# Attention stage: where the next pair's q and k products stand, and the order of copies in the last two pairs

## The reference

```python
q, k, v = jnp.split(x @ w_in, 3, axis=-1)          # 16 heads of 64
q = q * 64 ** -0.5
s = einsum('bihd,bjhd->bhij', q_c, k_c) + bias      # bias by clipped distance, per head
p = softmax(where(valid, s, NEG_INF))
o = einsum('bhij,bjhd->bihd', p, v_c)
return o @ w_out
h = layer_norm(ALPHA * h + y, g, b)
```

## Time and profile before

| What | Value |
| --- | --- |
| Median of three executions | 1161.33 us |
| Profiled execution, its own time | 1161.39 us |
| Its span, first to last instruction | 1159.6 us |
| TensorE busy | 1150.3 us (99%) |
| VectorE, ScalarE, GpSimd busy | 706.2, 525.5, 406.3 us (61, 45, 35%) |
| Chain that ended last, TensorE's share | 98% |
| Granted TensorE clock, mean | 0.999 of full |
| Attention scores, first and last start | 623.9 and 757.4 us |

### The profile page before, as it was taken

The page is one execution under the profiler, slowest core; times in us unless marked ns, Lnnn a source line. Parts: engine busy times, 40 slices in busy tenths (PEclk is TensorE's granted clock), DMA queues, the critical chain, the costliest instruction groups (busy, mean ns, idle before and its releaser), DMA issues.

```text
span 1159.6 us, 18903 instructions
## 1 busy us (share of the span) xinstructions
PE 1150.3 (99%) x6960; PEld 1020.4 (88%) x6960; DVE 706.2 (61%) x1178; ACT 525.5 (45%) x918; POOL 406.3 (35%) x240
## 2 busy tenths in 40 slices
PE   9999999999999999999999999999999999999997
PEld 7888888989999998888887878788999999998886
DVE  5070173789888873443504667757888888844436
ACT  4355253335555554332415565762355555543222
POOL 2539425141111115446145443551311111144441
PEclk9999999999999999999999999999999999999999
DMA  6533314242223334325032212141223333333221
GB/s 221 179 130 109 109 37 146 77 143 96 92 103 109 109 109 145 107 75 181 20 109 73 91 47 91 46 166 53 73 73 110 109 109 109 109 125 115 87 73 73
DMA packets 21976, 119.89 MB, mean 103 GB/s; under 512 B 2448, under 2 KB 6672, under 8 KB 8992
## 3 DMA queue, kind: packets, MB, share of 16 engines
q1 hardware_dynamic: 15440, 104.96, 25.6%
q10 hardware_dynamic: 6480, 14.17, 3.5%
HBM read 117.02 MB, written 5.24 MB: 105 GB/s over the span
## 4 chain that ended last, share of the span: by engine, by line
PE 98%; issue 0%; ACT 0%; DVE 0%; POOL 0%; DVEq 0%; POOLq 0%; ACTq 0%
PE bank L1765 29%; PE bank L1767 29%; PE bank L1766 29%; PE bank L2176 2%; PE bank L2160 2%; PE bank L1796 1%; PE bank L1848 1%; PE bank L2197 1%; PE bank L2196 1%; PE bank L2047 1%; PE bank L2040 0%; PE bank L2055 0%; PE bank L1986 0%; PE bank L2033 0%; PE bank L1992 0%
## 5 line engine op out<-in xcount | busy, mean ns | idle before, releaser
L1046 POOL TENSOR_TENSOR s_w_lo<-s_raw,s_w_hi 128x1024 fp32r<-128x1024 f32 x104 | 257.2, 2482 | 280.1 <-ACT s_w_hi L531 280.1
L1765 PE MATMUL bank<-s_t_hi,s_w_hi 128*128 128x256 f32 (+1 forms) x832 | 264.4, 318 | 0.0
L1766 PE MATMUL bank<-s_t_lo,s_w_hi 128*128 128x256 f32 (+1 forms) x832 | 262.8, 316 | 0.0
L1767 PE MATMUL bank<-s_t_hi,s_w_lo 128*128 128x256 f32 (+1 forms) x832 | 262.8, 316 | 0.0
L531 ACT ACTIVATE s_w_hi<-s_raw 128x1024 fp32r<-128x1024 f32 x111 | 116.3, 1059 | 219.1 <-PE bank L1767 188.0
L1071 POOL TENSOR_TENSOR s_w_lo<-s_raw,s_w_hi 128x512 fp32r<-128x512 f32 x36 | 64.3, 1785 | 305.1 <-ACT s_w_hi L631 305.1
L1767 PEld LDWEIGHTS bank<-s_t_hi,s_w_lo 128*128 128x128 f32 x832 | 158.6, 191 | 10.1
L1765 PEld LDWEIGHTS bank<-s_t_hi,s_w_hi 128*128 128x128 f32 x832 | 158.7, 191 | 9.7 <-issue 0.2
L1766 PEld LDWEIGHTS bank<-s_t_lo,s_w_hi 128*128 128x128 f32 x832 | 158.7, 191 | 9.4
L1297 DVE TENSOR_TENSOR s_a_lo<-s_act_a,s_a_hi 128x512 fp32r<-128x512 f32 x44 | 84.7, 1939 | 108.8 <-ACT s_a_hi L599 108.6
L1765 PE MATMUL bank<-s_w_hi,s_a_hi 128*128 128x512 f32 x352 | 137.2, 390 | 0.0
(11 more groups left out here) (218 smaller groups left out, 2074.7 us busy)
## 6 DMA issues: line engine op xcount, KB each, us to landing
s_raw<-stream SPq DMA_DIRECT2D x97, 1024.0 KB, 4.7
s_ln_gb<-ln_gb ACTq DMA_DIRECT2D x4, 1024.0 KB, 6.5
bias_rows<-rel_bias ACTq DMA_DIRECT2D x1, 3072.0 KB, 12.2
s_h<-x ACTq DMA_DIRECT2D x1, 2048.0 KB, 12.7
s_r_b<-bias_rows ACTq DMA_DIRECT2D x16, 128.0 KB, 3.4
s_x_t<-x_t ACTq DMA_DIRECT2D x3, 512.0 KB, 9.2
out<-s_h SPq DMA_DIRECT2D x3, 512.0 KB, 2.6
s_x_t<-x_t ACTq DMA_DIRECT2D x2, 256.0 KB, 5.7
```

Of the source, the lines that this page charges most:

```text
L1046: nc.gpsimd.tensor_tensor(lo, raw[:, place // 2 % RAWS, n % 2, :], hi.bitcast(F32), ALU.subtract).then_inc(lo_done, 2 if n == 1 else 1)
L1765: nc.tensor.matmul(out, l_hi, r_hi, start=start, stop=False, skip_group_check=skip)
L1766: nc.tensor.matmul(out, l_hi, r_lo, start=False, stop=False, skip_group_check=skip)
L1767: return nc.tensor.matmul(out, l_lo, r_hi, start=False, stop=stop, skip_group_check=skip)
```

## The change

Four things are moved; no instruction is added or removed, and what is computed stays.

- **Pieces on TensorE.** From the second pair on, the next pair's eight q pieces all stand in the first round, and the eight k pieces of the pair after it all in the third; the second round has none. Pair 0 has 5, 3 and 8, with 8 ahead of it; pair 6 has 5 and 3.
- **Copies.** ScalarE makes k's high half at the start of the first round and q's at the start of the second (in pair 0 behind the exponentials), and splits a slab at the end of each of the two. VectorE makes k's low half behind the first maxima and q's behind the second; from pair 1 on the low halves of units 0 and 1 stand ahead of tile 2's division and those of units 2 and 3 behind it.
- **Early parts.** In round 21 parts 2, 3 and 4 all stand ahead of the turns, where part 2 did before and parts 3 and 4 behind them.
- **Last two pairs.** VectorE takes the maxima of round 21 ahead of the low halves of round 19 and alternates head sums and low halves; ScalarE makes the high halves of round 21 ahead of `pair_high(4)` and `pair_high(5)`.

```diff
             def first_round(r, p):
+                k_high(p + 1)
                 exponents(here[0])
...
                     load_bias(p + 1)
+                split_hi(RPA_KQ + 2 * (p + 1) + RING)
             def second_round(r, p):
-                k_high(p + 1)
+                if p >= 1:
+                    q_high(p + 1)
                 for s in range_of(r):
                     exponents(s)
+                if p == 0:
+                    q_high(p + 1)
                 for s in range_of(r - 1):
                     weights_high(s)
                 if p >= 1:
                     head_half(2 * p - 2)
                     head_half(2 * p - 1)
-                split_hi(RPA_KQ + 2 * (p + 1) + RING)
-            def third_round(r, p):
-                q_high(p + 1)
+                split_hi(RPA_KQ + 2 * (p + 1) + 1 + RING)
+            def third_round(r):
                 for s in range_of(r - 1):
                     weights_high(s)
                 for s in range_of(r):
                     exponents(s)
-                split_hi(RPA_KQ + 2 * (p + 1) + 1 + RING)
...
             first_round(r - 2, p)
-            k_high(p + 1)
-            split_hi(RPA_KQ + 2 * (p + 1) + RING)
...
             pair_high(3)
             for s in range_of(r + 1):
                 exponents(s)
+            for s in range_of(r):
+                weights_high(s)
             pair_high(4)
             pair_high(5)
-            for s in range_of(r):
-                weights_high(s)
...
                 maxima(r)
+                k_low(p + 1)
                 if p >= 1:
                     lows(r - 1)
                 divide(r)
                 maxima(r + 1)
-                k_low(p + 1)
-                divide(r + 1)
-                lows(r)
                 if p >= 1:
+                    q_low(p + 1)
+                    weights_low(range_of(r)[0])
+                    weights_low(range_of(r)[1])
+                    divide(r + 1)
+                    weights_low(range_of(r)[2])
+                    weights_low(range_of(r)[3])
                     head_sum(2 * p - 2)
                     head_sum(2 * p - 1)
+                else:
+                    divide(r + 1)
+                    q_low(p + 1)
+                    lows(r)
                 maxima(r + 2)
-                q_low(p + 1)
                 lows(r + 1)
                 divide(r + 2)
             p, r = RPA_PAIRS - 2, HEADS_FROM
             maxima(r - 2)
+            k_low(p + 1)
             lows(r - 3)
             divide(r - 2)
             maxima(r - 1)
-            k_low(p + 1)
...
             divide(r)
-            lows(r - 1)
             p, r = RPA_PAIRS - 1, HEADS_FROM + 1
             maxima(r)
+            lows(r - 2)
             head_sum(2 * p - 4)
+            weights_low(range_of(r - 1)[0])
             head_sum(2 * p - 3)
-            lows(r - 1)
+            weights_low(range_of(r - 1)[1])
...
-            PIECES = {0: (0, 6), 2: (0, 3), 3: (0, 7)}
-            FIRST_PIECES = {0: (0, 5), 2: (1, 4), 3: (0, 6)}
-            LEAD = 7
-            LAST_PARTS = {HEADS_FROM: ((0, 1), ()), HEADS_FROM + 1: ((2,), (3, 4)), HEADS_FROM + 3: ((), (5, 6, 7))}
+            PIECES = {0: (0, 8), 2: (0, 0), 3: (0, 8)}
+            FIRST_PIECES = {0: (0, 5), 2: (1, 2), 3: (0, 8)}
+            LAST_PIECES = {0: (0, 5), 2: (0, 3), 3: (0, 0)}
+            LEAD = 8
+            LAST_PARTS = {HEADS_FROM: ((0, 1), ()), HEADS_FROM + 1: ((2, 3, 4), ()), HEADS_FROM + 3: ((), (5, 6, 7))}
```

More of the change, by code:

```diff
@@ L970, in _ @@
                 second_round(PER_PAIR * p + 1, p)
-                third_round(PER_PAIR * p + 2, p)
+                third_round(PER_PAIR * p + 2)
             p, r = RPA_PAIRS - 2, HEADS_FROM
             first_round(r - 2, p)
-            k_high(p + 1)
-            split_hi(RPA_KQ + 2 * (p + 1) + RING)
             for s in range_of(r - 1):
@@ L2232, in _ @@
                     scores(p, t)
-                beside, behind = (FIRST_PIECES if p == 0 else PIECES)[tiles[0]]
+                beside, behind = (FIRST_PIECES if p == 0 else PIECES if p < RPA_PAIRS - 2 else LAST_PIECES)[tiles[0]]
                 if r == HEADS_FROM:
```

## The result

The changed kernel takes 1165.0 us (median of 7, 1164.6 to 1165.6), before 1161.33 in the same measurement (1160.89 to 1161.51). The ratio is 1.0032, 95% interval 1.0022 to 1.0042: slower by 3.7 us. The forecast was 1166.6, slower by 5.3.

What follows compares the result with a forecast made beforehand. The prediction took TensorE, busy for 99% of the span, as the bound. Its terms summed as 1161.39 + 2.9 + 1.6 + 0.8 = 1166.7, against the median 1166.6 us, with a range of 1162.5 to 1170.0.

Steps and rivals of the forecast that it cites:

- Steady pairs: Pairs 1 to 5: TensorE waits 0.68 before unit 5's turn, less 0.1 for a saved switch; +2.9 us over five pairs.
- The sign that I set: Pairs 1 to 5: five TensorE waits of 0.5 to 0.8 before unit 5's turn, and a period of 19.2.
- The saved switch: Pairs 1 to 5: removing the second round's block of three pieces saves a matmul switch, 0.1 us a pair, bounds 0 and 0.2.
- the lower bound: Pairs 1 to 5: even with divisions costing nothing, a wait of 0.3 stays; with 0.2 saved, +0.1 us a pair.
- Pair 0: Tile 2's turns wanted 1.4 us earlier, q_high ahead of the high halves: waits of 1.4 and 0.25, +1.6 us.
- Pairs 6 and 7: Pair 7: part 4 waits 0.4 for GpSimd, then late turns, exponentials and tile 2's scores; +0.8 us, bounds -1.1 and +1.5.
- up to 0.3: Pair 7: high halves ahead of pair_high(4) and (5) win back up to 0.3 us.
- Cost 0 of the rest: Pairs 1 to 5: other moved copies, slab splits and loads are covered and cost 0, unless GpSimd's work falls on a division.
- Rival (a): Pairs 1 to 5: GpSimd's low half of k's slab blocks the division, net 1.15 a pair, 1169.5 us; chance 0.18.
- Rival (b): Shorter chain, divisions overlapped, pairs 0 and 7 neutral: +0.1 to +0.3 a pair, about 1 elsewhere, 1163.2 us; chance 0.12.
- Rival (c): Faster: 0.2 of switches saved in each of five pairs, pair 7's three waits (1.1) gone, 1159.2 us; chance 0.12.

Runs made afterwards that it cites:

- x1_cover: The changed kernel with three of the third round's eight k pieces back in the second round, behind the V products: 1163.18 us, ratio 1.0017.
- x5_divfirst: The changed kernel with VectorE, from pair 1 on, dividing tile 2 ahead of the low halves of units 0 to 3: 1164.48 us, ratio 1.0027.
- x6_parts: The changed kernel with only round 21's early parts as before (3 and 4 behind the turns), VectorE's new list kept: 1164.35 us, ratio 1.0025.
- x10_actonly: The kernel before with only ScalarE's high halves of round 21 moved ahead of pair_high(4) and (5): 1161.02 us, ratio 0.9998.
- x7_all: The changed kernel with pieces 8, 3, 5 (pair 0: 5, 1+4, 6), early parts and VectorE's last-two-pairs list as before: 1160.91 us, ratio 0.9996.
- x8_pool: The kernel before with GpSimd's third output slab low half ahead of the last bias, ScalarE's round 21 high halves ahead of pair_high(4), (5): 1160.24 us, ratio 0.9989.

## Why the prediction was right, and where its sizes were off

**Steady pairs (forecast +2.9, measured +1.71).** The mechanism was the one named: unit 5's turn, the low half of unit 3, no cover. x1_cover shows that with the cover back all of it goes. The sign that I set, waits of 0.5 to 0.8 and a period of 19.2, was not met: the wait is 0.44 by the starts (0.2 in the view of waits) where I had 0.68, and the period 18.97. Mis-sized was the end of the chain, 5.65 behind tile 2's scores instead of 5.89: I gave the divisions 0.81, from a pair in which GpSimd's bias ran beside them, and the low halves in front of them their whole duration, 0.62. They took 0.66 and 0.54 from start to next start, 0.23 less together, which is the whole difference. The saved switch was 0.1 as taken. x5_divfirst bears out the lower bound: with the division out of the way 0.13 a pair comes back, and the rest of the wait remains, since the high half of unit 2 stands behind the V products.

**Pair 0 (+1.6, measured +1.40).** Both parts were right, and the times of the single steps are within about 0.2: q's copy starts 3.74 behind tile 2's scores (forecast 3.78), and the wait is 1.22 by the starts (1.14 in the row; forecast 1.4). What I did not say is that the pieces alone undo it.

**Pairs 6 and 7 (+0.8, measured +0.73, less 0.16 behind).** The size fitted, partly by luck, as the account was incomplete. The forecast chain is in the trace of after: parts, late turns, late exponentials, late scores; part 4's wait was 0.24, not 0.4. But of VectorE's new order I counted only the earlier exponentials, which "no longer decides", and the later maxima. I left out that the low halves of tile 2, for which the turns wait, now stand behind the maxima; x6_parts shows that this alone keeps tile 2's scores as late. The 0.16 behind tile 3's scores is the "up to 0.3" for the earlier high halves, which gave 0.26 in x10_actonly.

**Cost 0 of the rest.** Right: x7_all.

**Rival (a)** did not come in after, for the reason given: the bias starts 5.3 to 5.8 us after the pair's start, in pairs 1 to 5, instead of 6.5 to 7.3, so that GpSimd's weight half is through before the division. In pair 2 the weight load is now issued 4.5 us ahead of the bias load (658.17 and 662.63) instead of 1.7. Its mechanism is real: in x5_divfirst, where the division is earlier, it struck one pair of five and cost 0.37. Rival (b), about 1163.2, was nearer to the measured size of the steady pairs than I allowed, but has pairs 0 and 7 neutral, which they are not. Rival (c) needed the low half of unit 3 before TensorE asks; it was 0.44 late.

## What to carry to other kernels

Work that fills a wait does not show as such while it does: before moving filler on the bounding engine, take its next wait, follow the chain that it hides to its end in the rows, and compare that end with the new time at which it is asked for. Use start-to-start times in such a chain, not durations, as consecutive short instructions overlap by a tenth of a us each. And a copy that waits for something late must not stand ahead of one that is ready and wanted: in-order lists turn one late input into everyone's.

## What the runs showed of the hardware

One GpSimd instruction on two operands in SBUF (a weight's low half, 2.4 us) holds up a VectorE division that reads and writes SBUF. In x5_divfirst the pair of divisions of 384 columns took 1.75 instead of 0.75, in before 1.82 instead of 0.88 at 512 columns, and 0.88 again once GpSimd's instruction was moved (x8_pool). The hold-up ended some 0.2 us ahead of the listed end of GpSimd's instruction. The added time was 0.94 where that instruction had 1.13 left to run (before), 1.00 where it had 1.20 left, and 0.06 to 0.07 where it had 0.26 to 0.27 left (pairs 3 and 5 of x5_divfirst, 0.81 and 0.82).

VectorE's subtraction from a PSUM bank beside the same GpSimd instruction did not slow (0.69 at 669.20, within 668.24 to 670.62, in after). GpSimd's one-operand bias instruction costs the divisions little: two of 384 columns took 0.86 to 0.89 in the five pairs of before in which it ran as they started (1 and 3 to 6), and 0.75 in pair 2, where it was through, and in all pairs of after.

The Trainium skill, "SBUF — State Buffer", section "SBUF: two separate sides", tells of an exclusive lock between the two engines: it is taken by any GpSimd instruction and by a VectorE one in a two-port mode or with two inputs in SBUF, and whichever comes later blocks fully. The first of these rows agrees, and so does the second, as the subtraction has one input in SBUF. The third it would make a full block too, and there the rows do not bear it out.
